# A twelve-stage fp32 block on one core: late sums of squares, local queries one step earlier, delta-rule convolutions respread, and other moves of order

## What is computed

```python
for i in range(DEPTH):                      # conv, fox, gdn, swa
    h = rms_norm(x, norm_w[i])
    x = x + mixer[i](h)
h = rms_norm(x, final_norm_w)
for i in range(DEPTH_2):                    # hgrn2, mla
    m = mixer_2[i](rms_norm_2(h, pre_mix_norm[i]))
    h = h + rms_norm_2(m, post_mix_norm[i])
    f = jnp.square(jax.nn.relu(rms_norm_2(h, pre_mlp_norm[i]) @ w1[i])) @ w2[i]
    h = h + rms_norm_2(f, post_mlp_norm[i])
    e, g = p[i] @ w_ple_proj[i], jax.nn.sigmoid(h @ w_ple_gate[i])
    h = h + rms_norm_2(g * e, ple_norm[i])
```

## Time and profile before

| what | value |
|---|---|
| median of 3 runs | 2809.57 us (2807.46 to 2810.58) |
| the profiled execution, its own time | 2810.84 us |
| its span in the trace | 2809.0 us |
| PE busy in the span | 2687.3 us (96%) |
| DVE, ACT, POOL busy | 1388.0, 1209.8, 1076.4 us |
| mean granted TensorE clock | 0.991 |

### The profile page before, as it was taken

One profiled execution on the slowest core, in us unless ns is written; L12 is line 12 of the kernel. 1 busy time (PEld: TensorE's weight loads), 2 busy tenths in 40 slices (PEclk: granted clock), 3 DMA queues, 4 the chain that ended last, 5 costly groups with the idle time before them and its releaser, 6 DMA issues.

```text
span 2809.0 us, 41976 instructions
## 1 busy us (share of the span) xinstructions
PE 2687.3 (96%) x13876; PEld 2142.5 (76%) x13876; DVE 1388.0 (49%) x2446; ACT 1209.8 (43%) x1879; POOL 1076.4 (38%) x803
## 2 busy tenths in 40 slices
PE   7999999899999899999999999999999999999998
PEld 6887777776767667778887788887677877788886
DVE  7335333677676667576665421127754353321126
ACT  4224443444444445455544432235554463332233
POOL 5544332433333332344335344444412313444442
PEclk9999999999999999999999999999999999999999
DMA  4322222211111221222222223332211202232231
GB/s 162 96 90 90 75 71 63 75 46 60 30 60 34 70 68 61 66 77 75 67 68 90 86 94 97 97 108 83 75 38 45 68 30 68 90 98 91 96 106 51
DMA packets 59640, 211.85 MB, mean 75 GB/s; under 512 B 6688, under 2 KB 7072, under 8 KB 59552
## 3 DMA queue, kind: packets, MB, share of 16 engines
q1 hardware_dynamic: 57744, 206.89, 23.4%
q10 hardware_dynamic: 1520, 2.75, 0.3%
q0 software_dynamic: 288, 1.05, 0.1%
HBM read 208.57 MB, written 2.10 MB: 75 GB/s over the span
## 4 chain that ended last, share of the span: by engine, by line
issue 38%; PE 36%; POOL 17%; DVE 8%; ACT 1%; DMA 0%; POOLq 0%; DVEq 0%; SPq 0%; ACTq 0%
POOL weights_low L371 17%; PE bank L1292 10%; PE bank L1294 10%; PE bank L1293 10%; DVE work L1728 2%; PE bank L1395 1%; PE bank L1061 1%; PE bank L1081 1%; DVE activations_low L451 1%; DVE work L1725 1%; DVE work L965 0%; DVE work L963 0%; PE bank L1377 0%; DVE to_split L676 0%; PE bank L1070 0%
## 5 line engine op out<-in xcount | busy, mean ns | idle before, releaser
L371 POOL TENSOR_TENSOR weights_low<-weights_raw,weights_high 128x512 fp32r<-128x512 f32 x776 | 1047.6, 1372 | 1580.1 <-ACT weights_high L355 1562.3
L1292 PE MATMUL bank<-activations_high,weights_high 128*128 128x512 f32 x2912 | 1186.5, 407 | 45.3 <-POOL weights_low L371 17.9
L1294 PE MATMUL bank<-activations_high,weights_low 128*128 128x512 f32 x2912 | 1143.4, 393 | 0.0
L1293 PE MATMUL bank<-activations_low,weights_high 128*128 128x512 f32 x2912 | 1142.2, 392 | 0.0
L1292 PEld LDWEIGHTS bank<-activations_high,weights_high 128*128 128x128 f32 x2912 | 551.5, 189 | 183.8 <-issue 20.4
L1294 PEld LDWEIGHTS bank<-activations_high,weights_low 128*128 128x128 f32 x2912 | 550.5, 189 | 117.4
L1293 PEld LDWEIGHTS bank<-activations_low,weights_high 128*128 128x128 f32 x2912 | 552.1, 190 | 110.5 <-issue 8.4
L355 ACT ACTIVATE weights_high<-weights_raw 128x1024 fp32r<-128x1024 f32 x384 | 404.0, 1053 | 300.7 <-PE bank L1294 293.3
L2818 DVE TENSOR_TENSOR mixed<-bank,mixed 128x512 f32 (+1 forms) x48 | 33.2, 692 | 193.9 <-PE bank L1294 193.9
L2762 ACT ACTIVATE to_split<-work 128x512 f32<-128x512 f32 x64 | 40.5, 632 | 185.7 <-DVE work L2804 185.7
L2804 DVE SCALAR_TENSOR_TENSOR work<-bank,rstd 128x512 f32<-128x512 f32 x64 | 44.2, 690 | 149.3 <-PE bank L1294 140.4
(11 more groups left out here) (442 smaller groups left out, 3245.1 us busy)
## 6 DMA issues: line engine op xcount, KB each, us to landing
weights_raw<-weights SPq DMA_DIRECT2D x388, 512.0 KB, 3.5
out_t<-residual SPq DMA_DIRECT2D x8, 256.0 KB, 2.0
residual<-x_t ACTq DMA_DIRECT2D x2, 512.0 KB, 7.6
residual<-x_t POOLq DMA_DIRECT2D x2, 512.0 KB, 10.5
work<-p_t ACTq DMA_DIRECT2D x2, 512.0 KB, 4.7
const<-consts SPq DMA_DIRECT2D x1, 713.0 KB, 12.7
const<-consts SPq DMA_DIRECT2D x1, 321.0 KB, 11.7
root<-positions ACTq DMA_DIRECT2D x1, 256.0 KB, 3.3
```

The source lines that it names most:

```text
L371: K.nc.gpsimd.tensor_tensor(K.w_lo[:, s, part], K.raw[:, s, part], K.w_hi[:, s, part].bitcast(F32), ALU.subtract).then_inc(K.job_sems["low ...
L1292: K.nc.tensor.matmul(dst, wh, K.act_hi[:, t, :], start=k == 0, stop=False)
L1293: K.nc.tensor.matmul(dst, wh, K.act_lo[:, t, :], start=False, stop=False)
L1294: ins = K.nc.tensor.matmul(dst, wl, K.act_hi[:, t, :], start=False, stop=k == len(tiles) - 1)
```

## The change

It alters the order of instructions in several stages and, in four joints, how the sum of squares is formed:

- **Joints.** In `hg_post`, `ple0_post`, `mla_post` and `ple1_post`, DVE adds six squares. The last two go to PE, as matmuls that accumulate behind that of `root`. The `weight_high` behind the joint moves ahead of the last square. In the `ple` joints the last square is made by DVE.
- **End.** Of the last eight tiles, five are formed on PE: identity times residual, plus identity times the product, copied out by ACT. DVE adds the other three.
- **Fox.** The first score tile and one part come ahead of the transposes of v.
- **Gdn.** DVE reads `qk` one level earlier. The four convolution steps for v are taken 2, 1, 1 behind levels 1, 2, 3 (they were 2, 2 behind levels 1 and 2). Those for the next head are taken 2, 2, 1, 1, 2 (they were 2, 2, 3, 1). The SiLU of v moves from level 3 to level 4. At the stage's end the product with z comes ahead of that with the root.
- **Swa.** PE runs the gate job and then the query job of the next but one step. At the last two steps the output jobs fill in, and `begun.finish()` replaces `out_pe`.
- **Embedding gate.** Two `weight_high` move by a tile. The rope sines move behind the fourth gate job.
- **Latent pairs.** The two products of the first rope job of `mla` run chunk by chunk together, each chunk as its tile of `mla_cq` is there.

```diff
+LATE_SQUARES = 2
 def stat_tensor(e, stage, fill=None):
     if stage in SUMMED:
-        keep_busy(e, 3)
-        e.eng.wait_ge(K.sem("square_used"), FIRST_SQUARE[stage] + n)
-        K.nc.tensor.matmul(K.ps[STAT_BANK][:, :], K.c("ones")[:, 0:P], K.root[:, :], start=True, stop=True) \
+        first = FIRST_SQUARE[stage]
+        e.eng.wait_ge(K.sem("square_used"), first + n - LATE_SQUARES)
+        K.nc.tensor.matmul(K.ps[STAT_BANK][:, :], K.c("ones")[:, 0:P], K.root[:, :], start=True, stop=False) \
             .then_inc(K.sem("sum_ready"), 1)
-        keep_busy(e, 5)
+        take(fill, 1) if fill else keep_busy(e, 1)
+        for t in range(first + n - LATE_SQUARES, first + n):
+            e.eng.wait_ge(K.sem("square_ready"), t + 1)
+            K.nc.tensor.matmul(K.ps[STAT_BANK][:, :], K.c("ones")[:, 0:P], K.sq[:, t % 2, :], start=False,
+                               stop=t == first + n - 1).then_inc(K.sem("square_used"), 1)
+        take(fill, DT) if fill else keep_busy(e, 4)
...
 def ahead_act(e, phase, done=0):
+    if phase in SUMMED_BY:
+        for n in range(DT):
+            weight_high(e, c0 + n + AHEAD)
+            if n == DT - 1:
+                weight_high(e, c0 + DT + AHEAD)
+            square_tile(e, SUMMED_BY[phase], 0, n)
+        return
...
 def fox_pe(e):
-        evacuated(e, c0 + 2, i)
-        for t in range(QT):
-            ins = nc.tensor.transpose(tb[:, t * P:(t + 1) * P], b.v[:, t * P:(t + 1) * P], K.c("ident"))
...
+        scores(0)
+        take(fill, 1)
+        values()
...
 def gdn_act(e):
-            if l == 3:
+            if l == 4:
                 e.eng.wait_ge(K.sem("gdn_conv"), i * 3 + 3)
                 act(b.x[:, 2, :], b.t[:, 2, :], ACT.Silu).then_inc(K.sem("gdn_silu"), 1)
...
 def gdn_dve(e):
             v.transpose(flat_s, flat_t).then_inc(K.sem("gdn_s"), 1)
-            if l < 3:
-                take(conv_v, 2)
+            if l == 1:
+                ring.wait("qk", i)
+                ring.read("qk", v.tensor_tensor(b.qkt, by_block(ring.bank("qk")[:, :]), b.dt, ALU.mult))
+            if l < 4:
+                take(conv_v, (2, 1, 1)[l - 1])
...
-        take(conv, 3)
+        take(conv, 1)
...
 def swa_pe(e):
+    begun = Begun(e, "swa_out", "swa_y", 4)
+    out = begun.by_tiles(SWA_STEPS - 2)
+        after_next = swa_jobs(t + 1)[0] if more else None
+        fill = all_parts(job_parts(e, z), out if after_next is None else job_parts(e, after_next))
-        if more and t:
-            for _ in job_parts(e, next_q):
-                pass
-        fill = job_parts(e, z)
-        take(fill, 2)
+        take(fill, 10)
-    out_pe(e, "swa_out", "swa_y")
+    begun.finish()
...
 def ple_act(e, name, layer):
-        if k in (2, 5):
-            weight_high(e, gate + 2 + k // 5)
+        if k in (3, 4):
+            weight_high(e, gate + k - 1)
-        rope_sines(e, *mla_angles(K)[:2], ROPES_BEFORE)
+        if n == SLOTS - 1 and not nth:
+            rope_sines(e, *mla_angles(K)[:2], ROPES_BEFORE)
...
 def mla_pe(e):
-    first(0)
-    second_of(0)
+    for k in range(3):
+        split_wait(e, "mla_cq", k + 1)
+        product(e, cr, bank_of(e, cr)[:, :], [8 + k], k, k == 0, k == 2)
+        ins = product(e, cr, second.bank("second")[:, :], [8 + k], 3 + k, k == 0, k == 2)
+    second.written(ins)
...
+def tail_products(e, gate):
+    for k in range(TAIL_TILES):
+        e.eng.wait_ge(e.K.sem("tail_product"), k + 1)
+        e.K.nc.tensor.matmul(tail_bank(e.K, gate, k)[:, :], e.K.c("ident"), e.K.M[:, k, :], start=False, stop=True) \
+            .then_inc(e.K.sem("tail_sum"), 1)
```

More of the change, by code:

```diff
@@ L478, in keep_busy, with stat_tensor @@
         K.nc.tensor.matmul(K.ps[IDLE_BANK][:, :], K.c("ident"), K.c("ones"), start=True, stop=True)
-def stat_tensor(e, stage):
+LATE_SQUARES = 2
+SUMMED_LATE = ("hg_post", "ple0_post", "mla_post", "ple1_post")
+def stat_tensor(e, stage, fill=None):
     K, (n, _) = e.K, STAT_SIZE[stage]
@@ L513, in root_scalar @@
         K.nc.scalar.preload_act_table_set("natural_log_exp_and_others")
-    if stage in SUMMED:
+    if stage in SUMMED and stage not in SUMMED_LATE:
         e.eng.wait_ge(K.sem("sum_ready"), list(SUMMED).index(stage) + 1)
@@ L710, in __init__, with by_tiles @@
         self.parts = [job_parts(e, c0 + r, None, B_TILES) for r in range(n)]
+    def by_tiles(self, early):
+        for tiles in (range(early), range(early, HELD)):
+            for parts in self.parts:
+                for k in tiles:
+                    split_wait(self.e, self.split, k + 1)
+                    next(parts)
+                    yield
     def chunks(self):
@@ L1071, in transposed, with values @@
             ins.then_inc(K.sem("fox_t_ready"), 1)
-        for step, q, parts in ((scores, 0, 1), (scores, 1, 4), (transposed, 0, 2), (scores, 2, 3), (transposed, 1, 2),
+        def values():
+            evacuated(e, c0 + 2, i)
+            e.eng.wait_ge(K.sem("fox_t_used"), i * 5 + 1)
+            settle(e)
+            for t in range(QT):
+                ins = nc.tensor.transpose(tb[:, t * P:(t + 1) * P], b.v[:, t * P:(t + 1) * P], K.c("ident"))
+            ins.then_inc(K.sem("fox_t_ready"), 1)
+        scores(0)
+        take(fill, 1)
+        values()
+        for step, q, parts in ((scores, 1, 4), (transposed, 0, 2), (scores, 2, 3), (transposed, 1, 2),
                                (scores, 3, 4), (transposed, 2, 4), (transposed, 3, 2)):
@@ L1306, in all_parts @@
     for g in gens:
-        yield from g
+        for part in g:
+            yield part
 GC = 128
@@ L1882, in head @@
                 ins.then_inc(K.sem("gdn_state"), 1)
+                if c == 0:
+                    take(conv, 2)
                 if c == NG - 2:
@@ L2883, in ple_pe @@
     ring.wait_read("e6", nth)
-    stat_tensor(e, name + "_post")
+    if not nth:
+        stat_tensor(e, name + "_post")
+        return
+    for use in ("e5", "e7"):
+        ring.wait_read(use, nth)
+    for k in range(3):
+        evacuated(e, gate + 4 + k)
+    stat_tensor(e, name + "_post", tail_residuals(e, gate))
+    tail_products(e, gate)
 def ple_act(e, name, layer):
@@ L2921, in ple_act @@
             square(n - 1)
-    square(DT - 1)
+        if n == SLOTS - 1 and not nth:
+            rope_sines(e, *mla_angles(K)[:2], ROPES_BEFORE)
+    if gate + DT + AHEAD < N_JOBS:
+        weight_high(e, gate + DT + AHEAD)
     K.nc.scalar.preload_act_table_set("natural_log_exp_and_others")
     root_scalar(e, name + "_post", False)
-    if gate + DT + AHEAD < N_JOBS:
-        weight_high(e, gate + DT + AHEAD)
     if not nth:
         take(post_act(e, name, "mla_h", 0, lambda k: K.col("pre_mix_norm_2", DT + k), "mla"), DT)
+        return
+    for k in range(TAIL_TILES):
+        e.eng.wait_ge(K.sem("tail_sum"), k + 1)
+        act(K.X[:, k, :], tail_bank(K, gate, k)[:, :], ACT.Copy).then_inc(K.sem("tail_copied"), 1)
 def ple_dve(e, name, layer):
@@ L2942, in ple_dve @@
         v.tensor_tensor(K.M[:, n, :], ple_projected(K, n), K.M[:, n, :], ALU.mult).then_inc(K.sem("m_ready"), 1)
-        if n:
+        if 0 < n <= DT - LATE_SQUARES:
             sum_square(e, name + "_post", n - 1)
-    sum_square(e, name + "_post", DT - 1)
-    if nth:
-        post_dve(e, name, "ple_norm_2", layer * DT)
+    last = FIRST_SQUARE[name + "_post"] + DT - 1
+    e.eng.wait_ge(K.sem("m_ready"), M_DONE[name])
+    e.eng.wait_ge(K.sem("square_used"), last - 1)
+    e.eng.wait_ge(K.sem("square_ready"), last)
+    v.scalar_tensor_tensor(K.sq[:, last % 2, :], K.M[:, DT - 1, :], 1.0 / D, K.M[:, DT - 1, :], ALU.mult, ALU.mult) \
+        .then_inc(K.sem("square_ready"), 1)
+    if nth:
+        stat_vector(e, name + "_post")
+        for k in range(DT):
+            ins = v.scalar_tensor_tensor(K.M[:, k, :], K.M[:, k, :], K.col("ple_norm_2", layer * DT + k), K.rstd[:, :],
+                                         ALU.mult, ALU.mult)
+            if k < TAIL_TILES:
+                ins.then_inc(K.sem("tail_product"), 1)
+                continue
+            e.steps.step(ins)
+            e.steps.wait()
+            v.tensor_tensor(K.X[:, k, :], K.X[:, k, :], K.M[:, k, :], ALU.add).then_inc(K.sem("x_ready"), 1)
     else:
@@ L3021, in mla_pe @@
     job(e, c0 + 5)
-    split_wait(e, "mla_cq", 3)
     cr = FIRST_JOB["mla_rope"]
```

49 lines of the change are left out of this document (30 added, 19 removed).

## The result

The changed kernel takes 2772.73 us (median of 4 runs, 2771.2 to 2773.18), against 2810.01 for the kernel before (4 runs). The ratio is 0.9867, with a 95% interval of 0.9856 to 0.9879. The forecast was 2759. The change gained 37.3 us where 50.6 were expected. The measured time lies inside the prediction's wide range (2746 to 2774), by 1.3 us, and 2.7 above the one that it gave for its main case (2748 to 2770).

A forecast was written before the change was run, and what follows sets the result against it. PE, busy 2687.3 of 2809.0 us, bounds the kernel; only its standstills, lower-clock stretches and the time behind its last job can be won. Terms sum to 50.6: 2809.6 - 50.6 = 2759, range 2746 to 2774.

The forecast's parts named there:

- main case: The whole kernel: all terms hold and sum to 2759 us; chance 0.68, range by itself 2748 to 2770.
- Fox: Fox stage: the first score tile and one part cover the v transposes' wait for ACT's copy; 7.4 us.
- Gdn: Delta rule: four PE waits per head change, 9.0 us over eight heads (ends 0 and 16); stage's end 0.7.
- Gdn swaps one wait for another: Delta rule: SiLU's wait exceeds 1.0, or c = 1 waits the full 1.5; gain 1 instead of 9, 2767; chance 0.11.
- The terms for the SiLU: Delta rule: the transposes of v newly wait 0.9 to 1.0 us per head for the SiLU at level 4.
- Swa: Local attention: standstills at t = 0 and t = 7 are filled, winning 6.3 and 4.5 to 5.0; together 11.0 us.
- Joints: `hg_post` and `mla_post`: POOL's `weight_high` pair 3 us earlier shortens PE's wait for DVE by 2.0 each, 4.0 us.
- three clock terms: The three joints before `ple1_post`: half-rate stretches behind the standstills go, 1.7 each, 5.1 us, with 0 as other end.
- `ple0`: First embedding gate: waits for L451 (1.5) and L2919 (2.2) go, plus 2.4 at its joint; 6.2 us.
- the 2.4: `ple0_post`: 2.0 from POOL's earlier pair, 0.4 from DVE making the last square; 1.0 less if they contend.
- `ple1` and the end: Second embedding gate's L451 wait goes (1.6), and five of the last eight tiles lose DVE's addition (3.5 in all); 5.1 us.
- Latent pair: First rope job of `mla`: its wait for L451 goes as chunks of both products follow the tiles; 2.1 us.

## Why the prediction was right, and where not

The time lay inside the wide range, near its end, and the sign and the mechanisms of most terms held. The forecast of 2759 was 14 us too low. Step by step:

- **Fox**, 7.4 forecast, 6.8 measured, right by its own steps in seven heads. In the first head, where 0.2 was allowed for, the score tile now stands 1.3 for DVE's `select_rows` (L1081), and the transposes had stood 0.9 there before. That is the 0.6 that is missing.
- **Gdn**, 9.0 + 0.7 forecast, 3.7 measured. This is the step that failed. Its size came near that of the rival "Gdn swaps one wait for another" (1 instead of 9), but neither of that rival's conditions came: the SiLU's wait is 1.01, and L1503 has no row. What came is the argument it gave, that DVE's times hang on what POOL does beside them. Three terms were wrong:
  - First, "with one fewer it is there some 1.2 earlier: 1.0 gone" took DVE's durations as fixed while an operation moved under POOL's pair. The mask went from 0.42 to 1.30, and the wait stayed at 1.0. The run with kt's reads first showed it.
  - Second, the prediction saw that the wait of the k transposes and the wait at L1865 share a chain, but took off only 0.35 to 0.45 per head for it. The two runs that take v's steps and qk's read back show that with v's steps as they were the whole 0.6 only moves (0.58 + 1.01, or 1.62 in one).
  - Third, L1496 has a new wait of 0.4 that I had not seen. It comes with v's steps: both runs with these back have no such row, and the one with the early table load still has it.

  The terms for the SiLU (1.0 forecast, 1.01 measured) and for L1503 (1.4 less a remainder; its row is gone) held. So of the moves within a head, that of the next head's steps carries the whole gain (by what is left; it was not undone alone): with the others undone the lead over the delta rule and its output is 8.0 + 2.0, with them 2.3 + 1.4.
- **Swa**, 11.0 forecast, 9.9 measured. t = 0 was 6.4 of 6.3. The standstill for the eighth tile was 2.18 of 2.3. The half rate behind it was under-sized: 1.7 instead of 0.5. The code does not settle whether it comes: of the eight kernels with this code at the stage's end, four have it.
- **Joints** `hg_post` and `mla_post`, 3.7 each with the clock, 3.5 and 3.6 measured. POOL's pair carries them, as forecast. Behind the joints the changed kernel's trace has no half rate. But eight of the ten experiments have a stretch of 3.41 us at 0.50 some 25 us behind `hg_post`, which costs 1.5, so one of the three clock terms is not safely won.
- **`ple0`**, 7.9 forecast with its joint and its clock, 5.8 measured. (1.5 + 2.2 + 2.4 is 6.1 and not 6.2, so 7.8 by its own terms.) By the count of matmuls the two waits of the gates gave 3.1 of 3.7, and the joint with its clock 2.7 of 4.1. DVE and PE there show why the 2.4 was mis-sized:

```profile
1930.29 1.78 DVE L557 TENSOR_TENSOR root<-root,squares 128x512 f32<-128x512 f32 x1
...
1931.99 1.78 DVE L3018 TENSOR_TENSOR mixed<-work,mixed 128x512 f32<-128x512 f32 x1
...
1933.69 0.68 DVE L557 TENSOR_TENSOR root<-root,squares 128x512 f32<-128x512 f32 x1
...
1934.52 1.10 PE L496 MATMUL bank<-root,const 128*128 128x512 f32 x2 [1.12 <-DVE root L557]
1935.01 0.69 DVE L3025 SCALAR_TENSOR_TENSOR squares<-mixed 128x512 f32<-128x512 f32 x1
...
1935.58 1.27 POOL L374 TENSOR_TENSOR weights_low<-weights_raw,weights_high 128x512 fp32r<-128x512 f32 x1 [2.35 <-ACT weights_high L358]
```

  Two DVE operations ahead of the sixth square's sum take 1.78 beside POOL. Idle matmuls covered that before; now PE stands for the sum, 1.12. The contention of the new DVE square (L3025), priced at 1.0 in the prediction, did not come: it issued 0.57 before POOL and took 0.69. That the wait at L496 explains the joint's miss is argued from these rows; no run tried it.
- **`ple1` and the end**, 5.1 forecast and 5.1 to 5.2 measured, but by luck: the gates gave 0.9 of 1.6 and the end 2.6 of 3.5, and the 1.6 that made up for it is a stretch at half rate in the kernel before (3.41 us from 2405), which was in no term of the forecast.
- **Latent pair**, 2.1 forecast, 2.2 measured.
- **Start and clock**. Over the first 268 us the changed kernel loses 1.9, though the code there is the same. The last section shows how much this differs between kernels with the same opening code. All eleven of them are behind the one trace of the kernel before, by 0.1 to 2.1, so a small effect of the change is not excluded. Another 1.1 went in the stage behind local attention, to a stretch at half rate that lies otherwise in each run.

The sum of the misses: 6.0 in the delta rule, 1.9 at the start, 2.1 in `ple0`, 1.1 in swa, 1.1 behind it, 0.6 in fox, and 0.4 at the joints, 13.2. Less 0.3 that the latent pair and the end won beyond their forecast, this is the 12.9 between 50.6 and the difference of the two spans, 37.7.

## What to carry to other kernels

An operation that is moved into the freed place may take another's time: before counting a saving on DVE, look for what POOL does at the new place and put there what reads a bank. Two waits on one chain are not two gains; and a wait merged from two short ones can cost more than both, by the clock behind it. Parts taken ahead to fill a standstill must have their weights, and the jobs behind them too.

## What the runs showed of the hardware

- A standstill of PE of 1.62 ahead of one of its products was followed by a granted clock of about 0.5 over 3.41 us in five of seven heads. With qk's read back, standstills of 0.58 and 1.01, apart by 5 us, were followed by none in the heads from 640 to 880.
- The stretches at half rate behind a joint or a stage's end come and go between kernels that have the same code there: behind local attention the lead changes by -1.7 in the changed kernel, -0.1 in the run with qk's read back, and in the stage behind it by -1.1 and +0.2 (and by +1.5 to +1.6 in four others). Differences under some 3 us between two profiled executions need the count of matmuls by stage.
- The first microseconds differ between kernels with the same opening code. In the changed kernel's trace the job matmuls start 0.43 apart until 19.1, as they do elsewhere at a granted clock of 0.50, where those of the kernel before start 0.23 apart from 13.6 on:

```profile
15.70 0.63 PE L1324 MATMUL bank<-activations_low,weights_high 128*128 128x512 f32 x1
16.13 0.63 PE L1325 MATMUL bank<-activations_high,weights_low 128*128 128x512 f32 x1
```

By 268 us the lead against the kernel before was -1.9 in the changed kernel, and between -0.1 and -2.1 in the ten experiments, which open alike. The one at -0.1 has the 0.23 of the kernel before at that place, and the other nine have the 0.43 for a longer or shorter while.
